# Decode loop of a hybrid attention step: probability copies moved from VectorE to ScalarE, compressed values moved past the probability transposes

## The reference

```
def _compress(k, pe, w1, b1, w2, b2):          # blocks of 32 positions, stride 16: 127 of them
    ...
    return jax.nn.gelu(flat @ w1 + b1) @ w2 + b2
...
ck = _compress(k_cmp, ...); cv = _compress(v_cmp, ...)
p_cmp = softmax(q . ck)                        # also ranks the blocks of the selected branch
o_cmp = p_cmp @ cv
o_sel = softmax over the selected blocks @ v_sel
o_win = softmax over the window @ v_win
o_a   = softmax over the 3 best blocks and the own one @ v       # MoBA
```

## Time and profile before

| what | value |
|---|---|
| median of 3 runs | 1215.67 us (1213.83 to 1218.47) |
| the profiled execution | 1212.21 us, its span 1210.4 us |
| TensorE busy over the span | 1082.5 us (89%) |
| VectorE, ScalarE busy | 539.9 us (45%), 528.4 us (44%) |
| TensorE's mean granted clock | 0.923 of full speed |

### The profile page before, as it was taken

How to read it: one execution, slowest core, us unless ns; L and a number is a source line. 1 busy time by engine, 2 the same in 40 slices (tenths; PEclk the granted TensorE clock), 3 DMA queues, 4 the chain that set the end, 5 groups by cost and what they waited for, 6 DMA issues and landing times. The chain is left out here.

```text
span 1210.4 us, 25547 instructions
## 1 busy us (share of the span) xinstructions
PE 1082.5 (89%) x9313; PEld 936.2 (77%) x9313; DVE 539.9 (45%) x1200; ACT 528.4 (44%) x1018; POOL 82.6 (7%) x59
## 2 busy tenths in 40 slices
PE   7889987678899898989898989978999799999996
PEld 3668865567687776778686868767999699999995
DVE  1500025524536363454636363656556645554314
ACT  3322224644545545555555554453443444433212
POOL 1234310000010100000000100000000000000000
PEclk9789986769899998999998999978999799999998
DMA  9788758128374664748383846563655154444401
GB/s 328 203 295 274 240 177 307 81 96 295 116 283 153 217 216 145 241 134 278 99 300 105 295 137 225 165 191 94 209 200 173 39 170 139 139 143 169 140 0 44
DMA packets 129908, 219.49 MB, mean 181 GB/s; under 512 B 19348, under 2 KB 74129, under 8 KB 125058
## 3 DMA queue, kind: packets, MB, share of 16 engines
q1 hardware_dynamic: 124962, 185.14, 46.7%
q0 software_dynamic: 4896, 33.68, 7.5%
HBM read 210.46 MB, written 12.45 MB: 184 GB/s over the span
## 5 line engine op out<-in xcount | busy, mean ns | idle before, releaser
L103 PE MATMUL ps<-b_uH,b_slabH 128*128 128x320 f32 x480 | 151.8, 316 | 11.9 <-DVE b_uL L547 7.5
L1207 PE MATMUL ps<-t_XT,t_slab 128*128 128x128 f32 x1024 | 145.4, 282 | 11.2 <-DVE t_XT L1632 9.7
L104 PE MATMUL ps<-b_uL,b_slabH 128*128 128x320 f32 x480 | 150.4, 313 | 0.0
L105 PE MATMUL ps<-b_uH,b_slabL 128*128 128x320 f32 x480 | 149.6, 312 | 0.0
L1207 PEld LDWEIGHTS ps<-t_XT,t_slab 128*128 128x128 f32 x1024 | 129.3, 195 | 22.9 <-issue 11.5
L2157 DVE TENSOR_TENSOR b_slabL<-t_slab,b_slabH 128x2048 fp32r<-128x2048 f32 (+1 forms) x52 | 109.1, 2124 | 62.2 <-ACT b_slabH L2054 62.2
L2054 ACT ACTIVATE b_slabH<-t_slab 128x2048 fp32r<-128x2048 f32 (+1 forms) x52 | 92.4, 1783 | 99.7 <-PE ps L105 92.8
L1492 ACT ACTIVATE t_KTr<-ps 128x512 f32<-128x512 f32 x152 | 82.4, 594 | 48.5 <-PE ps L1316 26.6
L103 PEld LDWEIGHTS ps<-b_uH,b_slabH 128*128 128x128 f32 x480 | 91.8, 191 | 14.5 <-issue 11.6
L104 PEld LDWEIGHTS ps<-b_uL,b_slabH 128*128 128x128 f32 x480 | 92.1, 192 | 0.0
L105 PEld LDWEIGHTS ps<-b_uH,b_slabL 128*128 128x128 f32 x480 | 92.0, 192 | 0.0
(11 more groups left out here) (383 smaller groups left out, 2131.8 us busy)
## 6 DMA issues: line engine op xcount, KB each, us to landing
t_Kr<-cache_moba_kv SPq DMA_DIRECT2D x132, 256.0 KB, 3.0
t_Vr<-cache_moba_kv SPq DMA_DIRECT2D x124, 256.0 KB, 5.7
t_slab<-w_ada SPq DMA_DIRECT2D x22, 1024.0 KB, 7.6
t_slab<-w_gu SPq DMA_DIRECT2D x22, 1024.0 KB, 5.3
t_slab<-w_in SPq DMA_DIRECT2D x17, 1024.0 KB, 6.4
t_slab<-w_down SPq DMA_DIRECT2D x11, 1024.0 KB, 5.2
t_slab<-cmp_w SPq DMA_DIRECT2D x2, 2048.0 KB
t_wkv<-cache_nsa_win SPq DMA_DIRECT2D x8, 512.0 KB, 3.3
```

The lines of the kernel that those rows point to most:

```text
L103: pe.matmul(out, w_high, x_high, start=start, stop=False, **kw)
L104: pe.matmul(out, w_high, x_low, start=False, stop=False, **kw)
L105: return pe.matmul(out, w_low, x_high, start=False, stop=stop, **kw)
L1207: return pe.matmul(out[:, P * j:P * j + P], taps(w, j, lp)[:, P * ht:P * ht + P], XT[:, w, lp, j, :, :].rearrange("p v i -> p (v i)"), sta ...
```

## The change

The job list and its owners: `hidden(1, 1)` moves behind `psel` and `pwin`; `values` moves into the second half; a new job `cout` gets a bank for the compressed value product, which was in bank 6 with the other outputs. `psel` and `pwin` leave `BY_DVE` and are so emptied by ScalarE.

```
-              + [("hidden", 1, 1), ("psel", 0, 0), ("psel", 1, 0), ("pwin", 0, 0), ("values", 0, 0)]
-              + [("pmoba", q, 0) for q in range(4)])
-STEADY = FRONT_JOBS + [("pown", 0, 0)] + NSA_JOBS + [("final", 0, 0)]
-LAST = FRONT_JOBS + [("pown", 0, 0), ("final", 0, 0)]
+              + [("psel", 0, 0), ("psel", 1, 0), ("pwin", 0, 0), ("hidden", 1, 1)]
+              + [("pmoba", q, 0) for q in range(4)] + [("pown", 0, 0)])
+STEADY = FRONT_JOBS + NSA_JOBS[0:3] + [("values", 0, 0)] + NSA_JOBS[3:5] + [("cout", 0, 0)] + NSA_JOBS[5:12] + [("final", 0, 0)]
+LAST = FRONT_JOBS + [("values", 0, 0), ("cout", 0, 0), ("final", 0, 0)]
```

```
                 ring(it, ("hidden", 1, 1))
-                hidden_values(it, 1, range(0, 24), True)
+                hidden_values(it, 1, range(0, 16), False)
...
+                hidden_values(it, 1, range(16, 24), True)
-                wait_emptied(it, ("hidden", 1, 1))
+                pe.wait_ge(hid_added, it * 3 + 3)
...
-                bank = ring(it, ("values", 0, 0))
-                pe.wait_ge(cmp_act, it * N_ACT_CMP + 4)
...
-                probabilities(it, 0)
-                probabilities(it, 1)
-                wait_emptied(it, ("values", 0, 0))
...
-                probabilities(it, 2)
-                probabilities(it, 3)
+                for q in range(4):
+                    probabilities(it, q)
                 own_probabilities(it)
...
                 hidden_keys(it, it + 1, 0)
+                compressed_values(it)
                 segments(1)
                 moba_values(it, 1)
+                compressed_products(it)
```

```
                 keys(it, 2)
+                act.wait_ge(hidden_mm, it * 2 + 2)
+                middle(0, ps[6])
                 keys(it, 3)
...
+                for n in range(2):
+                    act.wait_ge(filled, nth(it, ("psel", n, 0)))
+                    copy(PTs[:, 4 * n:4 * n + 4, :]..., ps[...][:, :]).then_inc(emptied_act, 1)
+                act.wait_ge(filled, nth(it, ("pwin", 0, 0)))
...
+                copy(PTw[0:NCMP, 0, :], bank[0:NCMP, 0:64])
+                copy(PTw[:, 1:5, :]..., bank[:, 64:320])
+                copy(PTw[0:64, 5:7, :]..., bank[0:64, 320:448]).then_inc(emptied_act, 1)
+                if more:
+                    act.wait_ge(scored, it * N_SCORE + N_SCORE)
+                    stage_queries(it + 1)
+                    relay_quarter(it, it + 1, 0)
                 act.wait_ge(filled, nth(it, ("hidden", 1, 1)))
-                middle(0, ps[6])
                 middle(1, ps[...])
+                act.wait_ge(weights_ready, it + 1)
+                exp(t["sweight"][:, :], ...).then_inc(cmp_act, 1)
                 act.wait_ge(max_done, it * N_MAX + 4)
                 exp(Sm[:, OWN:OWN + 64], ...)
...
                     odd_segments(it, 0, 1)
+                act.wait_ge(*hidden_added(it))
+                gelu(1, 0)
+                gelu(1, 1).then_inc(cmp_act, 1)
+                if more:
                     act.wait_ge(out_mm, it * N_OUT + 2)
                     keep_quarter(0)
```

```
+                add_hidden(it, 1, 0, ps[6])
                 take_keys(it, 2)
                 take_keys(it, 3)
+                dve.wait_ge(small_mm, it * N_SMALL + 4)
+                dve.tensor_copy(t["sstat"][:, 2:4], ps[7][:, 0:2]).then_inc(small_taken, 1)
...
-                add_hidden(it, 1, 0, ps[6])
-                add_hidden(it, 1, 1, ps[...]).then_inc(emptied_dve, 1)
-                for n in range(2): ...   (the psel copies; the three pwin copies behind them)
+                add_hidden(it, 1, 1, ps[...])
...
-                dve.tensor_copy(t["On"][:, 0, :], ps[6][0:64, 0:64])
...
+                    segment_differences(it, 0, 1)
+                    values_copy()
+                    segment_differences(it, 1, 0)
+                    segment_differences(it, 1, 1)
+                    products_copy()
```

More of the change, by code:

```diff
@@ L966 @@
               + [("key", q, hp) for q in range(1, 4) for hp in range(4)]
-              + [("hidden", 1, 1), ("psel", 0, 0), ("psel", 1, 0), ("pwin", 0, 0), ("values", 0, 0)]
-              + [("pmoba", q, 0) for q in range(4)])
-STEADY = FRONT_JOBS + [("pown", 0, 0)] + NSA_JOBS + [("final", 0, 0)]
-LAST = FRONT_JOBS + [("pown", 0, 0), ("final", 0, 0)]
+              + [("psel", 0, 0), ("psel", 1, 0), ("pwin", 0, 0), ("hidden", 1, 1)]
+              + [("pmoba", q, 0) for q in range(4)] + [("pown", 0, 0)])
+STEADY = FRONT_JOBS + NSA_JOBS[0:3] + [("values", 0, 0)] + NSA_JOBS[3:5] + [("cout", 0, 0)] + NSA_JOBS[5:12] + [("final", 0, 0)]
+LAST = FRONT_JOBS + [("values", 0, 0), ("cout", 0, 0), ("final", 0, 0)]
 RING = (0, 1, 4, 5)
-BY_DVE = ([("hidden", 1, 1)] + [("key", q, 0) for q in range(3)] + [("psel", 0, 0), ("psel", 1, 0), ("pwin", 0, 0), ("values", 0, 0), ("pown", 0, 0),
+BY_DVE = ([("hidden", 1, 1)] + [("key", q, 0) for q in range(3)] + [("values", 0, 0), ("cout", 0, 0), ("pown", 0, 0),
                                                ("final", 0, 0), ("pmoba", 0, 0), ("pmoba", 2, 0)]
@@ L1264, in hidden_values @@
                     last = product(out, 1, ht, n // 8, n % 8, n % 8 == 0, n % 8 == 7)
-                if ht and final:
-                    last.then_inc(filled, 1)
+                if final:
+                    last.then_inc(filled if ht else hidden_mm, 1)
             def moba_values(it, q):
@@ L1322, in own_probabilities, with compressed_values, compressed_products @@
                 pe.transpose(bank[0:64, 0:P], Sm[:, OWN:OWN + 64], ident[:, :]).then_inc(filled, 1)
+            def compressed_values(it):
+                bank = ring(it, ("values", 0, 0))
+                pe.wait_ge(cmp_act, it * N_ACT_CMP + 4)
+                for kv in range(KV):
+                    for ht in range(2):
+                        last = pe.matmul(bank[0:NCMP, DH * kv:DH * kv + DH], hid[:, ht, P * kv:P * kv + NCMP],
+                                         t["w2"][:, 1, ht, :], start=ht == 0, stop=ht == 1)
+                last.then_inc(filled, 1)
+            def compressed_products(it):
+                bank = ring(it, ("cout", 0, 0))
+                wait_emptied(it, ("values", 0, 0))
+                apart(pe, turns)
+                for kv in range(KV):
+                    last = pe.matmul(bank[32 * kv:32 * kv + 32, 0:64], PTw[0:NCMP, 0, 32 * kv:32 * kv + 32],
+                                     cv[0:NCMP, DH * kv:DH * kv + DH], start=True, stop=True)
+                last.then_inc(filled, 1)
             def sequence(it, more):
@@ L1400, in sequence @@
                 for kv in range(KV):
[L1401 removed]
+                    last = pe.matmul(ps[6][32 * kv:32 * kv + 32, 64:128], PTw[0:64, 5, 32 * kv:32 * kv + 32],
                               rows[:, 640 + DH * kv:640 + DH * kv + DH], start=False, stop=True)
[L1403 to L1417 removed]
                 last.then_inc(out_mm, 1)
[L1419 to L1420 removed]
+                for q in range(4):
+                    probabilities(it, q)
                 own_probabilities(it)
@@ L1641, in add_hidden @@
                                   .to_broadcast([P, 2, KV, NSEG // 2]), ALU.add)
-                if w:
-                    return last
-                last.then_inc(hid_added, 1)
+                last.then_inc(emptied_dve if w and ht else hid_added, 1)
             def add_taps(w, lps):
@@ L1736, in sequence @@
                 dve.tensor_scalar(t["mbias"][:, :], t["mbias"][:, :], t["mmax"][:, 0:1], None, ALU.add).then_inc(max_done, 1)
-                add_hidden(it, 1, 0, ps[6])
[L1739 to L1756, removed]
-                                  ps[RING[STEADY.index(("values", 0, 0)) % 4]][0:NCMP, 0:P].rearrange("p (v e) -> p v e", v=KV),
-                                  t["b2"][0:NCMP, :].unsqueeze(1).to_broadcast([NCMP, KV, DH]), ALU.add).then_inc(emptied_dve, 1)
-                probability_copy(dve, dve.tensor_copy, it, 0).then_inc(emptied_dve, 1)
+                add_hidden(it, 1, 1, ps[RING[STEADY.index(("hidden", 1, 1)) % 4]])
                 dve.wait_ge(cmp_act, it * N_ACT_CMP + 3)
@@ L1787, in sequence @@
                     segment_differences(it, 3, 1)
+                else:
+                    values_copy()
+                    products_copy()
                 dve.wait_ge(filled, nth(it, ("final", 0, 0)))
```

42 lines of the change are left out of this document (27 added, 15 removed).

## The result

The changed kernel takes 1167.23 us (median of 4 runs, 1163.87 to 1172.43); the kernel before took 1214.75 us beside it (4 runs, 1212.25 to 1218.47). The ratio is 0.961, with an interval of 0.9561 to 0.9659.

What follows compares the result with a forecast made beforehand. TensorE was taken as the bound, stalled twice per sample. Gains of 31.5 (seven samples) and 5.6 (last), less 7 for the clock, left 30 us: profiled 1212.2 to 1182.2, median 3.5 higher, so 1186 us; range 1174 to 1208.

Steps and rivals of the forecast that it cites:

- the clock: TensorE's granted clock around the four short waits for exponentials: charged 1.0 us per sample, 7 in all; bounds zero and 29.
- H to T0: From start of `hidden(1, 1)` products (H) to start of next sample's segment transposes (T0): 14.0 us predicted, 19.94 before.
- the sum without the clock term: Gain over the whole decode with no clock loss: 31.5 us for seven samples plus 5.6 for the last, 37.1.
- the old slow stretch: In sample 0 before the change, TensorE behind the stalls was said to be at 1.2 GHz for about 10.2 us.
- The moved work: Compressed values and their product, moved into the next sample's stretch: predicted to add 1.45 us of TensorE time per sample.
- The last sample: Eighth sample, to the end of its final transposes: 26.63 us before, predicted gain 5.6 us.
- the back block's first loads: Loads starting when `hidden(1, 1)` is done: about 12 us needed, 13.6 left, predicted in time by some 1.5.
- The clock falls and stays low: Rival: TensorE's clock falls in each sample and stays low; gain shrinks to 8 us, 1207.5; chance 0.18.
- ScalarE becomes the bound: Rival: ScalarE's list from `psel` to the last exponential runs 2 us later in seven samples; gain 16, 1200; chance 0.13.
- The gather is late: Rival: GpSimd's gather, held back by `keep_quarter(0)`, delays third-quarter segment transposes; 0.9 us to spare; 1229.5 at twice 7.2; chance 0.07.

Runs made afterwards that it cites:

- `keep_first`: The changed kernel with `keep_quarter(0)` ahead of the Gelu instead of behind it: 1163.94 us, ratio 0.9597 to the kernel before.
- `spread`: The changed kernel with the next sample's queries and two relay copies moved between the pairs of MoBA exponentials: 1186.68 us, ratio 0.9763 to the kernel before.
- `whole`: The changed kernel with all 24 products ahead of `psel`, copies still on ScalarE, values late: 1185.24 us, ratio 0.9763 to the kernel before.
- `one_wait`: The changed kernel with the first probability transposes waiting for all eight block exponentials, one wait in place of four: 1193.84 us, ratio 0.9855 to the kernel before.
- `u_values`: The changed kernel with compressed values and product back ahead of and between the probability transposes, Gelu straight behind the exponentials: 1221.93 us, ratio 1.0079 to the kernel before.
- `u_copies`: The changed kernel with `psel` and `pwin` copies back on VectorE, all 24 products ahead of `psel`, values late: 1183.7 us, ratio 0.9761 to the kernel before.

## Why the prediction was right in kind and wrong in size

**The steps that failed: the clock first, then the size of two terms.** I charged 1.0 us per sample, 7 in all, as a value between no fall and a fall in every sample. In its trace the changed kernel paid nothing: 1.00 in all windows of the decode, and H to T0 the same within 0.02 us. With that term alone at nothing the forecast would have been 1212.2 - 37.1 + 3.5 = 1178.6 us, still inside the range; the gain without the clock was put too small as well, in the places that follow. The evidence at hand was one stall of 1.79 us that cost the clock in sample 0 and not in sample 3; the new waits are a sixth of it. The low end of the range held the sum without the clock term and 4 us for small errors; three small errors of the same sign, 11 us together, used up more. The prediction also says that the old slow stretch ended 0.6 us into the slice at 335; a granted clock of 0.81 there means 0.4, and its length of 10.2 us is worked out from that.

**H to T0: 13.52 and not 14.0, 3.3 us in seven samples.** The order came out as told, with ScalarE's list a little earlier at each step:

| step, from H | predicted | measured |
|---|---|---|
| `psel` begins | 3.75 | 3.78 |
| `psel` copies done | 5.5 | 5.55 |
| `pwin` copies done | 6.5 | 6.39 |
| selected value products begin | 7.5 | 7.61 |
| exponentials begin | 8.85 | 8.49 |
| first, second, third, fourth transposes begin | 10.25, 11.25, 12.2, 13.2 | 10.06, 11.04, 11.93, 12.91 |
| T0 | 14.0 | 13.52 |

The `pwin` copies took 0.65 us and not 0.8, and from their end to the own rows' exponential it was 2.10 us, not 2.35. The copy that I took from the earlier trace rows measured 0.59 again.

**The moved work: 0.92 and not 1.45, 3.7 us in seven samples.** The values and the product take 0.83 and 0.21 us of TensorE's line up to the next row. The mean of 0.92 holds half a us that `keep_first` takes away, so the work itself added 0.42 net. In sample 0, `keep_first` against before, it is 0.56: of the 1.04, some 0.3 comes back in the rows next to the moved work, and 0.2 in a shorter wait of L1207 for VectorE's segment differences (0.49 in place of 0.67).

**The front: 4.0 us that are not the change.** The first segment transposes of the decode began at 265.39 before and 261.09 after, behind code that is the same in both. In the seven experiments, which share that code too, they began between 262.52 and 267.30. This part varies by several us from one trace to another, which fits the spread of the runs of one kernel (8.6 us for the changed one); what sets it is not shown. Without it the decode gained 44.3 us, and 1212.2 - 44.3 + 3.5 = 1171.4 would still lie below the range.

**The last sample: 5.99 and not 5.6.** From the end of the final transposes to the end of the span it is 405.9 us against 405.7, so the back block's first loads were in time.

With these, 30 + 7 + 3.3 + 3.7 + 4.0 + 0.4 = 48.4, and 48.3 were measured. That the median lies 3.5 us above the profiled run held (3.4).

**The rivals.** *The clock falls and stays low* did not happen; `spread` shows that it can, with waits of about 1 us, and what it costs then. *ScalarE becomes the bound* is true of the place and not of the price: all four waits left are for its exponentials, but it was early. VectorE is as near to being the bound there: its block choice ended at 319.83 + 0.23 = 320.06, and the exponentials began at 320.10, so in sample 0 a shorter list on ScalarE alone would not have started them sooner. *The gather is late* came true in small. GpSimd issued it at T0+4.47 and ScalarE's copies of it ended at 336.88 + 1.15 = 338.03, just ahead of the transposes at 338.09: 0.06 us to spare, not 0.9, mainly because the moved work pushed these transposes back by less than 1.45. (The prediction's T0+4.95 for the issue does not follow from the 3.5 and 2.1 beside it.) In samples 3 to 5 TensorE waited: 0.49 us in sample 3, 0.25 in sample 5, and twice in sample 4:

```profile
580.20 1.18 PE L1182 MATMUL ps<-t_ident,t_relay 128*128 128x128 f32 x8 [0.53 <-ACT t_relay L1503]
581.90 1.08 PE L1201 MATMUL ps<-t_KTr,t_qb_cur 128*64 128x512 f32 x4 [0.52 <-ACT t_KTr L1503]
```

`keep_first` takes these waits away but for one of 0.2 us, which ties them to the order of `keep_quarter(0)` and the Gelu.

The table load lasted 1.28 us and the Gelu ran at its end, 326.61 + 1.28 = 327.89 against 327.91. The Trainium skill, "ScalarE: Activation LUTs", section "What ACT_TABLE_LOAD costs", has a drain of about 1.38 us beside the load; the trace shows none, as before, and the row was the right one to take.

**What stays open.** Whether the clock stays up in every run of the changed kernel: its two longer runs have a mean granted clock of 0.941 and 0.943 (0.948 in the other two), and no trace shows in which part of the program. What separates the falls from the rest. In `spread`, `whole` and `one_wait` single waits are longer and the waits together are too, and within one kernel it fell in some samples and not in others. Why `u_values` is 10 us above the upper end of its expectation: the trace places about 7 of it. H to T0 is 20.73 us and not 20 at most, 5 us in seven samples, with the products behind the stall of 5.47 us at half clock (1.94 and 1.92 above), and from T0 to the next H it is 46.41 us and not 47.04 - 0.9, 2 us more; the rest is open. What the move of the copies is worth by itself in the changed order of products is open too.

## What to carry to other kernels

When an engine stands still twice in one stretch, look whether both waits hang on one list of another engine: here removing the first alone lengthened the second (`u_values`), and moving the last consumer behind other work paid (29 us in `u_copies`). Before a copy goes to another engine, look what is waiting behind it on that engine's list: `u_copies` and `whole` took the same time. Then put independent work of the waiting engine between the pieces that arrive one by one; here that, with the gather sent earlier, was worth another 10 us over the change. Give an uncertain clock term its own end of the range, without it, and add the small errors of the other terms to that end in full: they can have the same sign.

## What the runs showed of the hardware

The granted clock does not answer to one wait in a fixed way. The same wait of 3.16 us ahead of the same transposes left 1.97 us in one sample and 3.63 in another (`one_wait`), and the waits of 1.10 and 0.78 us left it at full in one sample of seven (`spread`). The Trainium skill, "TensorE: Matmul & The Clock Gate", section "A second HAM failure mode: psum-queue depth-cycling", says that frequent short idle pieces between groups of matmuls can make the clock swing; `spread` agrees (0.95 behind T0 in sample 4), and the changed kernel, with waits of 0.3 us at the same places, does not show it (1.00).
